# Feed-forward chunks with the weights stationary instead of the tokens

## What is computed

```python
D_MODEL = 1024; SEQ = 256; D_FF = 2816

def rms_norm(x, g):
    y = xf * lax.rsqrt(jnp.mean(xf * xf, axis=-1, keepdims=True) + EPS)
    return (y * g).astype(x.dtype)

def swiglu(x, w_in, w_out):
    gate, up = jnp.split(x @ w_in, 2, axis=-1)
    return (jax.nn.silu(gate) * up) @ w_out

# layer by layer, twice:
h = swiglu(rms_norm(x, g[0]), w_ffn_in[layer, 0], w_ffn_out[layer, 0])
x = x + 0.5 * rms_norm(h, g[1])
...
h = swiglu(rms_norm(x, g[4]), w_ffn_in[layer, 1], w_ffn_out[layer, 1])
x = x + 0.5 * rms_norm(h, g[5])
```

## Time and profile before

| | |
|---|---|
| median of three runs | 1389.88 us |
| profiled execution | 1390.04 us, span 1388.1 us |
| TensorE matmuls | 1366.6 us busy, 98% |
| GpSimd | 1135.2 us, 82% |
| ScalarE | 660.7 us, 48% |
| VectorE | 454.8 us, 33% |
| the loops of F0 and F1 | 134.4 and 134.3 us, 8 chunks a loop |

### The profile page before, as it was taken

How to read it: one execution, slowest core, us unless ns; L and a number is a source line. 1 busy time by engine, 2 the same in 40 slices (tenths; PEclk the granted TensorE clock), 3 DMA queues, 4 the chain that set the end, 5 groups by cost and what they waited for, 6 DMA issues and landing times.

```text
span 1388.1 us, 18203 instructions
## 1 busy us (share of the span) xinstructions
PE 1366.6 (98%) x6396; PEld 1119.7 (81%) x6396; DVE 454.8 (33%) x1134; ACT 660.7 (48%) x741; POOL 1135.2 (82%) x912
## 2 busy tenths in 40 slices
PE   6999999999999999999999999999999999999997
PEld 5888888888888888888888778888888877788886
DVE  6101134654000156311002884000156134552224
ACT  5444445546444455544443766444455434544531
POOL 5999977849999967998899449999978976679882
PEclk9999999999999999999999999999999999999999
DMA  7666554526655545665565426656554653446550
GB/s 251 211 209 203 188 199 144 196 92 228 200 193 182 182 167 186 206 211 182 183 194 196 136 70 213 192 189 192 193 167 154 211 173 130 126 148 228 185 178 31
DMA packets 160958, 246.95 MB, mean 178 GB/s; under 512 B 8924, under 2 KB 99844, under 8 KB 160772
## 3 DMA queue, kind: packets, MB, share of 16 engines
q1 hardware_dynamic: 158612, 239.42, 52.8%
q10 hardware_dynamic: 2288, 6.75, 1.4%
HBM read 245.10 MB, written 1.05 MB: 177 GB/s over the span
## 4 chain that ended last, share of the span: by engine, by line
POOL 59%; PE 22%; issue 17%; DMA 1%; ACT 1%; DVE 0%; POOLq 0%; ACTq 0%; SPq 0%; DVEq 0%
POOL w_lo L553 59%; PE acc L1858 5%; PE acc L1861 5%; PE acc L1859 5%; PE gu L2358 1%; PE gu L1858 1%; PE gu L1859 1%; PE gu L1861 1%; PE tb L2367 1%; PE tb L1861 1%; PE tb L1859 1%; PE tb L1858 1%; PE tb L2393 0%; DMA x_res<-in_x 0%; DMA w_raw<-in_w_in 0%
## 5 line engine op out<-in xcount | busy, mean ns | idle before, releaser
L553 POOL TENSOR_TENSOR w_lo<-w_raw,w_hi 128x512 fp32r<-128x512 f32 x896 | 1130.1, 1303 | 226.0 <-ACT w_hi L582 225.9
L582 ACT CAST w_hi<-w_raw 128x2048 fp32r<-128x2048 f32 x225 | 425.3, 1909 | 120.4 <-DMA w_raw<-in_w_ffn_in 32.8
L1858 PE MATMUL gu<-w_hi,xT_hi 128*128 128x512 f32 x832 | 330.6, 397 | 3.9 <-DVE w_lo L1782 2.8
L1859 PE MATMUL gu<-w_lo,xT_hi 128*128 128x512 f32 x832 | 324.4, 390 | 0.0
L1861 PE MATMUL gu<-w_hi,xT_lo 128*128 128x512 f32 x708 | 276.8, 391 | 0.0
L1858 PE MATMUL acc<-w_hi,xT_hi 128*128 128x512 f32 x496 | 198.2, 400 | 0.0
L1859 PE MATMUL acc<-w_lo,xT_hi 128*128 128x512 f32 x496 | 193.2, 390 | 0.0
L1858 PEld LDWEIGHTS gu<-w_hi,xT_hi 128*128 128x128 f32 x832 | 156.8, 188 | 35.7 <-DVE xT_lo L1184 3.2
L1861 PE MATMUL acc<-w_hi,xT_lo 128*128 128x512 f32 x468 | 182.7, 390 | 0.0
L1859 PEld LDWEIGHTS gu<-w_lo,xT_hi 128*128 128x128 f32 x832 | 157.0, 189 | 31.2 <-issue 0.2
L1861 PEld LDWEIGHTS gu<-w_hi,xT_lo 128*128 128x128 f32 x708 | 133.3, 188 | 28.6
(11 more groups left out here) (329 smaller groups left out, 1363.7 us busy)
## 6 DMA issues: line engine op xcount, KB each, us to landing
w_raw<-in_w_ffn_in SPq DMA_DIRECT2D x176, 512.0 KB, 4.7
w_raw<-in_w_ffn_out SPq DMA_DIRECT2D x88, 512.0 KB, 4.1
w_raw<-in_w_in SPq DMA_DIRECT2D x80, 512.0 KB, 4.5
w_raw<-in_mlstm_w_in SPq DMA_DIRECT2D x24, 512.0 KB, 4.6
w_raw<-in_w_ple_gate SPq DMA_DIRECT2D x16, 512.0 KB, 4.2
w_raw<-in_w_kv SPq DMA_DIRECT2D x16, 512.0 KB, 4.3
w_raw<-in_mlstm_w_out SPq DMA_DIRECT2D x8, 512.0 KB, 4.1
w_raw<-in_diff_w_q SPq DMA_DIRECT2D x8, 512.0 KB, 4.2
```

The costliest lines, as they stand in the source:

```text
L553: ins = pool.tensor_tensor(w_lo[:, slot.spl, cols], w_raw[:, slot.raw, cols], w_hi[:, slot.spl, cols].bitcast(F32), ALU.subtract)
L582: nc.scalar.copy(w_hi[:, slot.spl, :], w_raw[:, slot.raw, :]).then_inc(hi_ready, 1)
L1858: mm(out, xh, wh, start=(half == 0 and k == 0), stop=False)
L1859: mm(out, xh, wl, start=False, stop=False)
```

## The change

In the loops alone (8 of 11 chunks a block), the operands of gate and up change places. `gate_up_rows` takes four blocks of 128 weight columns (two of gate, two of up) as stationary operands; the transposed tokens move. `xT_hi` and `xT_lo` become the halves of one tile `xT`, so one matmul of 512 columns gives w_hi·x_hi in the bank's first 256 columns and w_hi·x_lo in its second; a matmul of 256 columns adds w_lo·x_hi to the first. Gate and up come out with **their columns on partitions**, one bank for each block of 128: `gu[:, 0]` and `tb[:, 1]` for gate, `gu[:, 1]` and `tb[:, 0]` for up.

So h needs no transpose, and `turn_h` leaves the loop. But `rstd` now differs along the columns: each block builds it as a row on all partitions once (`spread_rstd`, `turn_rstd` with two transposes, `take_row`), and VectorE adds the bank's two halves, each multiplied by that row (`whole`, in place in PSUM), before the silu and for up. ScalarE rounds up·silu straight out of PSUM into `hT_hi` or, in every second chunk, `hE_hi`.

```diff
-        xT_hi = sb("xT_hi", [P, KT, TILES * P], F32R)
-        xT_lo = sb("xT_lo", [P, KT, TILES * P], F32R)
+        xT = sb("xT", [P, 2, KT, TILES * P], F32R)
+        xT_hi, xT_lo = xT[:, 0], xT[:, 1]
...
+        def gate_rows(j):
+            return (gu[:, 0, :], tb[:, 1, :])[j]
+        def up_rows(j):
+            return (gu[:, 1, :], tb[:, 0, :])[j]
+        def h_rows(n):
+            return (hT_hi, hT_lo) if n % 2 else (hE_hi, hE_lo)
...
# ScalarE, in the loop instead of iteration(2 + d, i, At(s0 + 5 + 3 * d, i), True)
+                def by_rows(n, i, a):
+                    ahead(a)
+                    ahead(a.plus(1))
+                    for j in range(2):
+                        act.wait_ge(gate_scaled, i * 4 + row_count(f, n, 2, j))
+                        act.wait_ge(h_ready, i * 4 + (2 * NIT * f + 2 * (n - 1) + j + 1))
+                        nc.scalar.activation(sg[:, j, :], gate_rows(j)[:, 0:2 * P], ACT.Silu).then_inc(silu_ready, 1)
+                    ahead(a.plus(2))
+                    for j in range(2):
+                        act.wait_ge(h_ready, i * 4 + (2 * NIT * f + 2 * n + j + 1))
+                        nc.scalar.copy(h_rows(n)[0][:, j, :], up_rows(j)[:, 0:2 * P]).then_inc(row_hi_ready, 1)
...
# VectorE
+                def spread_rstd():
+                    for t in range(TILES):
+                        ins = v.tensor_scalar(rs_wide[:, t, :], ones[:], rstd[:, 2 * m + t:2 * m + t + 1], None, ALU.mult)
+                    ins.then_inc(rs_wide_ready, 1)
+                def take_row():
+                    dve.wait_ge(rs_row_in_psum, f + 1)
+                    v.tensor_copy(rs_row, tb[:, 1, 0:2 * P]).then_inc(rs_row_ready, 1)
+                def by_rows(n, i):
...
+                    def whole(rows, part, k):
+                        high, low = rows[:, 0:2 * P], rows[:, 2 * P:4 * P]
+                        v.tensor_tensor(part, low, rs_row, ALU.mult).then_inc(row_step, 1)
+                        v.tensor_tensor(high, high, rs_row, ALU.mult).then_inc(row_step, 1)
+                        dve.wait_ge(row_step, step(k))
+                        return v.tensor_tensor(high, high, part, ALU.add)
+                    for j in range(2):
+                        dve.wait_ge(gate_in_psum, i * 4 + row_count(f, n, 2, j))
+                        whole(gate_rows(j), row_part[:, j, :], 2 * j + 1).then_inc(gate_scaled, 1)
+                    for j in range(2):
+                        dve.wait_ge((tile0_used, slot_used)[j], At(s0 + 3 * n, i).count())
+                        whole(up_rows(j), row_part[:, j, :], 3 * j + 5).then_inc(row_step, 1)
+                        dve.wait_ge(row_step, step(3 * j + 6))
+                        dve.wait_ge(silu_ready, i * 4 + (2 * NIT * f + 2 * n + j + 1))
+                        u = up_rows(j)[:, 0:2 * P]
+                        v.tensor_tensor(u, u, sg[:, j, :], ALU.mult).then_inc(h_ready, 1)
+                    hi, lo = h_rows(n)
+                    for j in range(2):
+                        dve.wait_ge(row_hi_ready, i * 4 + row_count(f, n, 2, j))
+                        ins = v.tensor_tensor(lo[:, j, :], up_rows(j)[:, 0:2 * P], hi[:, j, :].bitcast(F32), ALU.subtract)
+                    ins.then_inc(ht_lo_ready, 1)
...
# TensorE
+                def gate_up_rows(n, i, a):
+                    for half in range(2):
+                        slot = a.plus(half)
+                        pe.wait_ge(lo_ready, slot.count())
+                        for r, rows in enumerate((gate_rows(0), gate_rows(1), up_rows(0), up_rows(1))):
+                            if half == 0 and r == 0:
+                                pe.wait_ge(h_ready, i * 4 + (2 * NIT * f + 2 * n))
+                            if half == 0 and r == 2:
+                                pe.wait_ge(ht_lo_ready, i * 2 + ht_count(f, n - 1))
+                            both = rows.rearrange("p (a c) -> p a c", a=2)
+                            for k in range(4):
+                                w = slice(512 * k + P * r, 512 * k + P * r + P)
+                                end = half == 1 and k == 3
...
+                                last = mm(both, w_hi[:, slot.spl, w], xT[:, :, 4 * half + k, :],
+                                          start=(half == 0 and k == 0), stop=end)
+                                if not end:
+                                    last = mm(rows[:, 0:2 * P], w_lo[:, slot.spl, w], xT_hi[:, 4 * half + k, :],
+                                              start=False, stop=False)
...
+                turn_rstd()
                 down_n(0, None, At(s0 + 4))
-                turn_h(1, None, hs_next if name in SKEWED else hs)
+                turn_h(1, hs_next if name in SKEWED else hs)
+                pe.wait_ge(rs_row_ready, f + 1)
                 with pe.Fori(0, (NIT - 3) // 2) as i:
                     for d in (0, 1):
-                        gate_up(2 + d, i, At(s0 + 5 + 3 * d, i))
+                        gate_up_rows(2 + d, i, At(s0 + 5 + 3 * d, i))
                         down_n(1 + d, i, At(s0 + 7 + 3 * d, i))
-                        turn_h(2 + d, i)
```

More of the change, by code:

```diff
@@ L1927, in ffn @@
                 f, s0 = FFN_NO[name], S[name]
-                def gate_up(n, turn, a):
-                    if n:
-                        pe.wait_ge(h_ready, 2 * NIT * f + 2 * n if turn is None else turn * 4 + 2 * NIT * f + 2 * n)
-                    across(a, 0, [gu[:, t, :] for t in range(TILES)])
-                    across(a.plus(1), 1, [gu[:, t, :] for t in range(TILES)])
+                def gate_up_rows(n, i, a):
[11 more added lines that the diff above has]
+                                end = half == 1 and k == 3
+                                if end:
+                                    mm(rows[:, 0:2 * P], w_lo[:, slot.spl, w], xT_hi[:, 4 * half + k, :],
+                                       start=False, stop=False)
[3 more added lines that the diff above has]
+                                    last = mm(rows[:, 0:2 * P], w_lo[:, slot.spl, w], xT_hi[:, 4 * half + k, :],
+                                              start=False, stop=False)
+                            if r >= 2:
+                                last.then_inc((tile0_used, slot_used)[r - 2], 1)
+                            elif half == 1:
+                                last.then_inc(gate_in_psum, 1)
@@ L1936, in down_n, with turn_rstd @@
                 def down_n(n, turn, slot):
                     pe.wait_ge(ht_lo_ready, ht_count(f, n) if turn is None else turn * 2 + ht_count(f, n))
+                    hi, lo = h_rows(n) if n else (hT_hi, hT_lo)
                     for t in range(TILES):
-                        down_tile(slot, hT_hi, hT_lo, t, n == 0, False)
-                def turn_h(n, turn, source=hs):
+                        down_tile(slot, hi, lo, t, n == 0, False)
+                def turn_rstd():
+                    pe.wait_ge(rs_wide_ready, f + 1)
+                    for t in range(TILES):
+                        ins = nc.tensor.transpose(tb[:, 1, tok(t)], rs_wide[:, t, :], ident[:])
+                    ins.then_inc(rs_row_in_psum, 1)
@@ L1944, in turn_h @@
+                def turn_h(n, source=hs):
                     if n == 0 and name in SKEWED:
@@ L1946, in turn_h @@
                     else:
-                        pe.wait_ge(h_ready, 2 * NIT * f + 2 * n + 2 if turn is None
-                                   else turn * 4 + 2 * NIT * f + 2 * n + 2)
+                        pe.wait_ge(h_ready, 2 * NIT * f + 2 * n + 2)
                     for k in range(2):
```

56 lines of the change are left out of this document (38 added, 18 removed).

## The result

The changed kernel took 1403.72 us, the median of four runs (1402.41 to 1404.86); beside it the kernel before took 1390.14 (1389.69 to 1391.36). The ratio is 1.0098, interval 1.0086 to 1.011: slower by 13.6 us, where 10 us less were forecast, and outside the range. The profiled execution took 1402.91 us (span 1400.9), 12.87 more than that of before.

What follows compares the result with a forecast made beforehand. TensorE was taken as the bound, busy without a gap in the loops at 16.786 us a chunk, to become 16.44. 1390.04 − 11.1 + 0.9 + 0.3 = 1380.1, so 1380.0 for the median; range 1376.4 to 1387.5 us.

Steps and rivals of the forecast that it cites:

- two small instructions fit: Block start, F1 and F3: VectorE spreads rstd between hT_lo's end at 335.60 and TensorE's turn_rstd at 336.40.
- Rival C: Loops: VectorE slows GpSimd's subtractions; at 1.42 us each still under the chunk's 16.44, at 1.7 1396 us; chance 0.02.
- The pair: Gate and up in the loops: a long matmul of 0.2267 us plus a short one of 0.117, 32 a chunk.
- That just fits under 0.117, with 5 ns to spare: Gate and up: loading 128 weight columns, 0.112 us, hides under a short matmul of 0.117 us.
- 11.1 us gain: Loops: 32 chunks, each 0.346 us shorter, 16.44 instead of 16.786, give −11.1 us.
- Rival A: Gate and up: short matmul doesn't hide a 128-column load; 1455 or 1437 us, no gain at 0.128; chance 0.09.
- mild case: Gate and up: a short matmul of 0.125 to 0.131 us, no change in time; chance 0.03.
- the far price: Gate and up: short matmul 0.19 us, 1455 us, or 16 bare loads a chunk, 1437 us; chance 0.06.
- F0's wait: F0's first chunks: TensorE waits once for an up bank behind ScalarE's DMA-delayed rounding; 0.3 us, between 0 and 1.5.
- their 0.465: Loops: four transposes of h and what they leave behind, 0.465 us a chunk, gone in 8 chunks a block.
- B: Loops: VectorE's row of 14 instructions gets late and TensorE waits 1.5 us a chunk; +48, 1428 us; chance 0.05.
- the forecast's 0.9 for the four: Start of each of four blocks: two more transposes, 2 × 0.11 us each, +0.9 us.

Runs made afterwards that it cites:

- e9: Changed kernel with rstd spread from PSUM, loads of all short and 24 of 32 long matmuls a chunk cut to 64 columns, products partly left out: 1381.64 us.
- e6: Changed kernel plus one unneeded VectorE copy of 256 columns out of PSUM ahead of the rstd spread in F1 and F3: 1403.89 us, ratio 1.0104.

## Why the prediction was wrong

**The step that failed first is four words: "two small instructions fit".** I had looked up when VectorE comes free (335.60) and when TensorE wants the result (336.40), and put nothing between but the instructions' length. I gave an instruction from SBUF to SBUF the length that it has alone, and no bounds. My own rows showed such instructions beside GpSimd: the second of the two of the earlier trace rows took 1.77 us, and I read them only for what they did to GpSimd. The trace of before has even the same operation, a `tensor_scalar` from SBUF to SBUF, eight times in the hybrid block (ns min/median/max):

```profile
L1651 DVE TENSOR_SCALAR arena<-arena,gcol x8: 342/345/1091, 1179.9 to 1238.5; 128x256 f32<-128x256 f32 x8
```

Six take 0.34 us, and the two beside GpSimd's subtractions 0.99 (at 1211.80) and 1.09 (at 1238.53). With that as a bound F3's wait could have been forecast. F1's could not: the longest beside a subtraction in that trace is 1.78 us. The price in the changed kernel was 0.28 to 11.30 us. At F1 that is +10.1 of wait and +1.3 of low clock behind it, at F3 +0.7.

The Trainium skill, "SBUF — State Buffer", section "SBUF: two separate sides", says that VectorE and GpSimd share a pair of ports as an exclusive lock, which a VectorE instruction in a two-port mode or with two SBUF inputs takes, and that whichever starts first has it for the whole instruction while the other "fully blocks". Whether this instruction, which has one SBUF tensor as input, runs in such a mode, no record here tells. The rows agree as far as F0, F2 and F3 go: at most one subtraction of 1.3 us. In F1 VectorE lost nine turns in a row, 11.30 us, which the page doesn't say can be.

**Rival C had the right two engines and the wrong loser.** It asked only whether VectorE slows GpSimd. GpSimd was not slowed, 1298 ns a subtraction against 1303 before; VectorE was stopped. And it looked at the loops, where each added instruction has an operand in PSUM, which is why there it was right: no group of VectorE's waits or lengths there was off.

**The pair: 344 ns forecast, 352 measured.** "That just fits under 0.117, with 5 ns to spare" was the right place to look and the wrong reading. The short one's own price was nearly right (118.3), but the long one next to it rose from 227 to 234, and I had charged a hidden load to the short one alone. The nearest rows of short matmuls had loads of 8 columns, the rows of 128-column loads stood under nothing but short ones; no row had both kinds in turn. 32 × 8.6 ns is 0.27 us a chunk, 8.7 us in all, and it left of the 11.1 us gain 2.4. The Trainium skill, "TensorE: Matmul & The Clock Gate", section "LDWEIGHTS (loading the stationary operand)", gives columns/1.2 ns for a load, 107 for 128 and 53 for 64. The records, 0.19 and 0.13 us, are longer and differ by about as much. Worked out from the page's figure, an estimate, a load of 128 columns fits under a short matmul of 118, as I had it; the runs show that pairs with such loads cost 8 to 9 ns more than the forecast's 344.

Rival A had the mechanism and a break-even "short one of 0.128", that is, a pair of 355 ns; at 352 the gain is nearly gone. The measured pair is at the edge of what I had as its mild case, a short one of 0.125 to 0.131 (a pair of 352 to 358), to which I gave 0.03; the far price had 0.06. e9 shows the other side: with small loads, and part of the product left out for them, the chunk is 16.46, near the forecast's 16.44, and the kernel 1381.6.

**F0's wait: 0.3 forecast, 1.7 measured.** The mechanism is the forecast's, the rounding of h behind a slot that ScalarE awaits from the DMA, but one chunk earlier than where I looked, and just outside my 0 to 1.5.

**What held.** The transposes cost their 0.465: the first chunk of a loop still contains the four of the chunk ahead of the loop, and takes 17.17 us where the others take 16.71. Nothing else but the price of a pair separates a chunk from the forecast. VectorE's row of instructions took 0.42 to 0.43 each, without a wait of TensorE, so B did not come. The rest of the kernel, 375.4 us of it behind F3, did not move.

The sum by its terms, as measured: 32 chunks at −0.074, −2.4; F1's wait 10.1 and its clock 1.3; F3's wait 0.7; F0's wait 1.7; and what is left of the stretches ahead of the blocks, 0.4, 0.5, 0.1 and 0.4, in place of the forecast's 0.9 for the four. Together +12.8 against +12.85.

## What to carry to other kernels

An instruction that VectorE gets from SBUF to SBUF has no known length while GpSimd streams: give it its source in PSUM, or another engine, where somebody waits for it, and count both engines as possible losers of a shared resource. When matmuls of half the length come between long ones, measure a pair and not one kind: a hidden load may be paid for by its neighbour. And a small gain in every turn of a loop is worth only as much as the few instructions added around it are known.

## What was not expected of the hardware

- A VectorE instruction of 0.28 us stood 11.30 us beside nine back-to-back instructions of GpSimd, and in three like places 0.6 to 1.3. GpSimd went on meanwhile at 1.220 us from start to start, faster than the 1.249 that it has in the loops. Moved by a copy (e6), the instruction stood 10.97 us.
- Ten microseconds of an idle TensorE cost 1.3 more, since the granted clock was 0.50 for the first 2.59 us of the chunk behind; in e6, where it was 0.50 for 5.76 us, F1's first chunk took 19.96 us for 18.49.
- The cost of loading 128 columns beside a short fp32r matmul appears on the long one: 234 for 227, and 228 with 64 columns for three of four. A weight load runs while the matmul before it streams in the same 128 rows of the array (a load at 100.32 beside a matmul from 100.31), and yet such pairs are not free.
- Grouped in fours, a long matmul that follows another long one still costs 225 to 236 ns, mean 231.3.
